# A two-block transformer kernel: expert weights cut across all four experts of a round, in runs of 4 KB, each slot released alone

## What is computed

```python
lg = (xt @ w_rg + b_rg)                      # group logits
g_sel = jnp.argmax(lg, axis=-1)
le = (xt @ w_re + b_re).reshape(t, N_GROUPS, EXPERTS_PER_GROUP)
top_l, top_i = lax.top_k(le_sel, TOP_K_IN_GROUP)
...
return (jax.nn.silu(xblk @ w1[e]) * (xblk @ w3[e])) @ w2[e]
```

## Time and profile before

| | us |
|---|---|
| median of 3 runs | 1914.07 |
| lowest, highest | 1911.24, 1917.08 |
| the profiled execution, its own time | 1911.82 |
| its span in the profile | 1910.1 |
| PE busy, share of the span | 1547.6 (81%) |
| DVE, ACT busy | 424.8 (22%), 248.6 (13%) |
| mean granted TensorE clock | 0.911 |
| HBM read, mean over the span | 708 MB, 371 GB/s |

### The profile page before, as it was taken

How to read it: one execution, slowest core, us unless ns; L and a number is a source line. 1 busy time by engine, 2 the same in 40 slices (tenths; PEclk the granted TensorE clock), 3 DMA queues, 4 the chain that set the end, 5 groups by cost and what they waited for, 6 DMA issues and landing times.

```text
span 1910.1 us, 23311 instructions
## 1 busy us (share of the span) xinstructions
PE 1547.6 (81%) x10212; PEld 745.9 (39%) x10212; DVE 424.8 (22%) x944; ACT 248.6 (13%) x531; POOL 86.8 (5%) x142
## 2 busy tenths in 40 slices
PE   7998777999998778989977667776799677677775
PEld 4754434764454434445522212222255222132222
DVE  2341111326431112463500000000043000000001
ACT  0310000126212011154100000000011000000000
POOL 1100000201100000112100000000000000000000
PEclk9999888999999899999988878888899888778888
DMA  8579999769979999299699999999977999999997
GB/s 288 202 274 423 423 423 416 288 251 388 352 284 416 420 421 413 91 366 383 244 424 423 424 424 423 423 424 424 420 325 315 424 424 424 423 424 424 423 424 288
DMA packets 129039, 711.11 MB, mean 372 GB/s; under 512 B 8377, under 2 KB 14505, under 8 KB 60321
## 3 DMA queue, kind: packets, MB, share of 16 engines
q1 hardware_dynamic: 122512, 697.14, 89.4%
q0 software_dynamic: 4320, 9.78, 1.5%
q10 hardware_dynamic: 2096, 2.57, 0.5%
HBM read 708.17 MB, written 1.05 MB: 371 GB/s over the span
## 4 chain that ended last, share of the span: by engine, by line
PE 46%; DMA 43%; DVE 6%; SPq 2%; ACT 2%; issue 2%; POOL 1%; DVEq 0%; PEldq 0%; ACTq 0%; POOLq 0%
DMA ring<-in_moe_w 23%; DMA ring<-in_moe_w_down 7%; PE pa L820 6%; PE pb L791 5%; DMA work<-in_moe_w 5%; DMA mod<-in_moe_w 4%; PE pa L838 3%; PE pb L768 3%; PE acc L1421 3%; PE acc L893 3%; PE acc L1416 2%; PE acc L1139 2%; DMA ring<-in_moe_w_up 2%; PE acc L1317 2%; DMA work<-in_moe_w_down 2%
## 5 line engine op out<-in xcount | busy, mean ns | idle before, releaser
L791 PE MATMUL pb<-ring,XT 128*32 128x512 f32 x1424 | 271.7, 714 | 89.1 <-DMA ring<-in_moe_w 89.0
L820 PE MATMUL pa<-ring,work 128*32 128x512 f32 x928 | 191.8, 754 | 65.3 <-DMA ring<-in_moe_w 41.5
L791 PEld LDWEIGHTS pb<-ring,XT 128*32 128x32 f32 x1424 | 61.7, 126 | 248.9 <-DMA ring<-in_moe_w 126.2
L838 PE MATMUL pa<-work,HM 128*128 128x128 f32 x1024 | 132.0, 291 | 17.6 <-issue 17.6
L939 DVE TENSOR_TENSOR work<-work,pb 128x256 f32<-128x256 f32 (+1 forms) x32 | 17.7, 554 | 576.1 <-PE pb L791 431.4
L893 PE MATMUL acc<-XT,work 128*128 128x512 f32 x256 | 118.4, 605 | 32.5 <-DVE XT L955 19.6
L838 PEld LDWEIGHTS pa<-work,HM 128*128 128x128 f32 x1024 | 130.5, 207 | 32.4 <-issue 32.4
L791 PE MATMUL pb<-work,XT 128*32 128x512 f32 x480 | 113.8, 697 | 26.4 <-DMA work<-in_moe_w 26.3
L768 PE MATMUL pb<-ring,XT 128*32 128x256 f32 x1600 | 110.2, 398 | 13.8 <-DMA ring<-in_moe_w_up 13.8
L820 PEld LDWEIGHTS pa<-ring,work 128*32 128x32 f32 x928 | 42.8, 132 | 175.8 <-issue 77.3
L902 ACT COPY XT<-pa 128x512 f32<-128x512 f32 x32 | 18.8, 586 | 596.8 <-PE pa L838 596.8
(11 more groups left out here) (416 smaller groups left out, 1795.8 us busy)
## 6 DMA issues: line engine op xcount, KB each, us to landing
ring<-in_moe_w SPq DMA_DIRECT2D x135, 2048.0 KB
work<-in_moe_w SPq DMA_DIRECT2D x46, 2048.0 KB
ring<-in_moe_w_up SPq DMA_DIRECT2D x28, 2048.0 KB
ring<-in_moe_w_gate SPq DMA_DIRECT2D x26, 2048.0 KB
ring<-in_moe_w_down SPq DMA_DIRECT2D x24, 2048.0 KB
ring<-in_w_mod SPq DMA_DIRECT2D x48, 1024.0 KB
mod<-in_moe_w SPq DMA_DIRECT2D x11, 2048.0 KB
work<-in_moe_w_down SPq DMA_DIRECT2D x8, 2048.0 KB
```

What stands on the lines that cost most here:

```text
L791: last = nc.tensor.matmul(hbank[m][j * CAP:(j + 1) * CAP, :], m_xg[:, k, j * CAP:(j + 1) * CAP], slot_of(s0 + j // 2)[:, at:at + fn], star ...
L820: last = nc.tensor.matmul(pa[j * CAP:(j + 1) * CAP, h, :], m_ht[:, c, j * CAP:(j + 1) * CAP], slot_of(i)[:, at:at + 512], start=(c == 0), ...
L838: last = nc.tensor.matmul(xg_ps[:, k, :], HM[:, tt, k * P:(k + 1) * P], m_p[:, tt, :], start=(tt == 0), stop=(tt == TT - 1))
```

## The change

Four edits go together.

1. `across` now holds for every round. Each slot has a quarter-width share of all four experts, four runs of 4 KB in a partition. In the narrow rounds slots 0 and 1 are the two halves of the gate's rows, 2 and 3 of up's, 4 and 5 of down's. In the wide rounds w1 and w3 have two such slots for each half of their rows. Each is waited for and given back by itself. The number and size of the transfers of expert weights stay, and so does the number of matmuls that use them. The extra warm-ups of round 7 stay in round 7 alone.
2. The router's DVE chain: the pick of the second expert and the sum of both picks become one instruction for each tile. The second pick by itself is then the difference, computed behind the release of PE.
3. The warm-ups before the wait for the picks are 10 and not 6.
4. `ab_w_in` comes in whole rows, in halves of a chunk, in order. PE starts with the first half chunk behind 3 warm-ups and waits for each further chunk in its first product.

```diff
 def across(fn, g, i):
     down = moe_slots(fn) - fn // P
-    if g == 0 and i < 2:
-        return 0, 0, i
-    if g == ROUNDS - 1 and i >= down:
+    if i < down:
+        return (i // 2, 0, i % 2) if fn == FN1 else (i // 2 % 2, i // 4, i % 2)
+    if i >= down:
         return 2, (i - down) // 2, (i - down) % 2
...
-            warm_tensor(pe, pb[:, 0, :], 6)
+            warm_tensor(pe, pb[:, 0, :], 10)
...
-                link(v.tensor_scalar(o2[:, t, :], tmp[:, t, :], at_, None, ALU.is_equal))
+                last = v.scalar_tensor_tensor(m_a[:, t, :], tmp[:, t, :], at_, o1[:, t, :], ALU.is_equal, ALU.add)
                 if t == 0:
-                    link(v.tensor_tensor(m_a[:, t, :], o1[:, t, :], o2[:, t, :], ALU.add))
-            v.tensor_tensor(m_a[:, t, :], o1[:, t, :], o2[:, t, :], ALU.add).then_inc(assign_ready, 1)
+                    link(last)
+            last.then_inc(assign_ready, 1)
+            dve.wait_ge(assign_ready, ph.moe + 1)
+            link(v.tensor_tensor(o2, m_a, o1, ALU.subtract))
...
-        def across_up_tensor(fn, rows, s0, bank, wait_full, free, slot_of, n, at_half=None):
-            for k in range(n):
+        def across_up_tensor(fn, rows, s0, k0, bank, wait_full, free, slot_of, n, at_half=None):
+            for k in range(k0, k0 + n):
+                i = s0 + (k - k0) // rows
...
-            if g == ROUNDS - 1:
+            if across(ph.fn, g, n_up):
                 for c in range(n_down):
-                    if c:
+                    if c and g == ROUNDS - 1:
                         warm_tensor(pe, pb[:, 1, :], 8)
...
-            for cols, signal in ((slice(2 * GW, AB_IN), lat_cols), (slice(0, 2 * GW), None)):
...
+            sp.dma_start(dst[:, 0:1, :], src[:, 0:1, :]).then_inc(first_chunk, 16)
+            sp.dma_start(dst[:, 1:2, :], src[:, 1:2, :]).then_inc(full[at[ph.slot0].slot], FILL)
+            stream_sync(sp, a["ab_w_in"][0], ph.slot0, 4, 2, AB_IN, 1)
...
-            pe.wait_ge(lat_cols, 64)
+            warm_tensor(pe, pb[:, 0, :], 3)
+            pe.wait_ge(first_chunk, 16)
             for k in range(KC):
+                if k == 1 or k and k % 2 == 0:
+                    slot_wait(pe, ph.slot0 + k // 2)
```

More of the change, by code:

```diff
@@ L743, in across_up_tensor @@
                 if k % rows == 0:
-                    wait_full(s0 + k // rows)
-                held = slot_of(s0 + k // rows).rearrange("p (j r f) -> p j r f", j=SIDE, r=rows)
+                    wait_full(i)
+                held = slot_of(i).rearrange("p (j r f) -> p j r f", j=SIDE, r=rows)
                 for j in range(SIDE):
@@ L782, in whole_up_tensor @@
                     if across(fn, g, s0):
-                        across_up_tensor(fn, KC // 4, s0, hbank[m], wait_full, free, slot_of, KC // 2)
+                        across_up_tensor(fn, KC // 4, s0, half * KC // 2, hbank[m], wait_full, free, slot_of, KC // 2)
                         continue
@@ L1250, in weights_of, with stream_sync @@
             return w[i * kk * P:(i + 1) * kk * P, cols].rearrange("(k p) c -> p k c", p=P)
-        def stream_sync(sp, w, q0, n, kk, width):
-            for i in range(n):
+        def stream_sync(sp, w, q0, n, kk, width, first=0):
+            for i in range(first, n):
                 dst = slot(q0 + i)[:, 0:kk * width].rearrange("p (k c) -> p k c", k=kk)
@@ L1862, in ab_sync @@
         def ab_sync(sp, ph):
-            for cols, signal in ((slice(2 * GW, AB_IN), lat_cols), (slice(0, 2 * GW), None)):
-                for i in range(4):
-                    q = ph.slot0 + i
-                    dst = slot(q)[:, 0:2 * AB_IN].rearrange("p (k c) -> p k c", k=2)[:, :, cols]
-                    src = weights_of(a["ab_w_in"][0], cols, 2, i)
-                    if signal is None:
-                        sp.dma_start(dst, src).then_inc(full[at[q].slot], FILL)
-                    else:
-                        sp.dma_start(dst, src).then_inc(signal, 16)
+            dst = slot(ph.slot0)[:, 0:2 * AB_IN].rearrange("p (k c) -> p k c", k=2)
+            src = weights_of(a["ab_w_in"][0], slice(0, AB_IN), 2, 0)
+            sp.dma_start(dst[:, 0:1, :], src[:, 0:1, :]).then_inc(first_chunk, 16)
+            sp.dma_start(dst[:, 1:2, :], src[:, 1:2, :]).then_inc(full[at[ph.slot0].slot], FILL)
+            stream_sync(sp, a["ab_w_in"][0], ph.slot0, 4, 2, AB_IN, 1)
             sp.wait_ge(b_small, 16 * B_SMALL)
@@ L1915, in ab_tensor @@
             for k in range(KC):
-                if k % 2 == 0:
-                    slot_wait(pe, ph.slot0 + k // 2)
                 for t in range(TT):
```

9 lines of the change are left out of this document (5 added, 4 removed).

## The result

| | before | after |
|---|---|---|
| median of 4 runs, us | 1912.65 (1908.96 to 1917.08) | 1928.84 (1928.54 to 1929.64) |
| span of the profiled execution, us | 1910.1 | 1927.4 |

The ratio is 1.0091, 95% interval 1.007 to 1.0113: the changed kernel is 16.2 us slower. The forecast was 1932.3, in a range of 1914 to 1946.

A forecast was written before the change was run, and what follows sets the result against it. The prediction took the saturated DMA stream of expert weights to bound the expert phases. Its terms, 25.8 - 0.4 (E1's idle time) - 2.5 - 1.9 - 1.8 - 1.0 = +18.2 us on 1914.07, gave 1932.3 us, range 1914 to 1946.

The forecast's parts named there:

- The bound and the mechanism: Expert phases: a full DMA queue sets their length, and shorter runs lower its rate; forecast chance 0.76.
- The rate: Expert-weight stream: 415 in place of 424 GB/s, 0.107 us more for each of 240 slots, 25.8 us.
- three short stretches: Stretches of 4 KB runs in the kernel before, at 421, 410 and 412 GB/s over 15, 14 and 10 us.
- the 410 and 412 stretches: Kernel before: 410 GB/s is half a mixer's weights, 412 expert weights; all at 410 would cost 41 us.
- The tails: Ends of E0 and E2: single slots let PE finish earlier, 0.6 and 1.9 us, sum -2.5 us.
- my clock rival: Phase ends: PE's bursts bring the lower clock to the tails, about 4 us each, 16 us, so 1948; chance 0.07.
- Parts 2 to 4: Router chain, warm-ups and kernel start: gains of 1.9, 1.8 and 1.0 us.
- the warm-ups' 1.8 us: Router of the wide phases: ten warm-ups shorten PE's idle gap and keep the clock, 0.9 us in each.
- a bracket: Warm-ups term: an aside that E1 and the gather behind may gain too, with no size given.
- The start: First product: starts near 11 us but needs the fourth chunk, so ends near 28.0 us, -1 us.
- The 421 rate: Rival, expert stream: 421 GB/s is the right rate, 8.4 us replace 25.8, so 1914.9, no change; chance 0.10.
- That run length costs nothing: Faster rival, expert stream: 423 GB/s or more in E2 and E3, only 7.2 us of gains, so 1906.9; chance 0.07.

The follow-up runs named there:

- Part 1 alone: Kernel before with only the 4 KB cut across four experts and single release of every expert slot; router, warm-ups and start unchanged: 1937.92 us, ratio 1.0151.
- the 4 KB runs alone: Kernel before with the same slots, experts and paired release, each slot's transfer issued as two so every run is 4 KB: 1942.86 us, ratio 1.0183.
- E2: Not a run: the first wide expert phase of the kernel, 444.92 us long before the change and 454.18 after.
- the rest alone: Changed kernel with the slot cut undone (8 KB runs, two experts); shorter router chain, ten warm-ups and new start stay: 1900.75 us, ratio 0.9957.
- E0: Not a run: the first narrow expert phase of the kernel, 207.44 us long before the change and 212.28 after.
- E3: Not a run: the last expert phase of the kernel, a wide one, 443.63 us long before the change and 453.29 after.
- E1: Not a run: the second narrow expert phase of the kernel, 213.49 us long before the change and 217.09 after.
- e4_16k_last: Kernel before with each slot of the last expert phase filled by one whole matrix in 16 KB runs, outputs differing: 1907.33 us, ratio 0.9974.

## Why the prediction was right

**The bound and the mechanism** held as written. The queue stays full, the rate falls, and the phases lengthen. Part 1 alone and the 4 KB runs alone both show it.

**The rate** was the term that mattered: 25.8 us, from a rate of 415 that I had averaged from three short stretches. Measured was 414. At 414 a slot takes 5.066 us, 0.120 more than at 424, and over the 240 slots that the forecast counted this is 28.8 us. The phases lost 27.4 in all, tails included. The count of the slots was right too: 4.8, 3.6, 9.3 and 9.7 us, where "about 9" and "3 to 4" were forecast. Taking the 410 and 412 stretches as seriously as the 421 one was what made it right. But the rate of 4 KB runs swings between 408 and 422 GB/s within a phase (below), and three short samples of it could have averaged some GB/s more or less. That they came so near to the mean was partly luck.

**The tails** were put too high: 2.5 us forecast. In E2 the way from the last up slot's products to those of the last down slot went from 21.91 to 21.17 us, so 0.7 and not 1.9. The forecast had the last down slot land 20.0 us behind the last up slot, as in the kernel before (20.01 us from arrival to arrival); in the changed one it is 21.18, because the last slot alone takes 6.3 us and not 5.1. It takes 6.2 with the rest alone too, so the run length isn't the reason; what is wasn't tried. E0 gave nothing, since the products of its last up slot and of its first down slot fell to the lower clock: 3.4 us more for both, of which 0.9 reached the end. This is the mechanism of my clock rival, but it cost time in this one place. In E2 and E3 the lower clock reached the first down slot as well, and the last transfer still set the end (waits of 2.26 and 1.00 us); the final additions took 3.70 us in E0, E2 and E3, before and after.

**Parts 2 to 4** were put too low: 4.7 us forecast, 10.0 by the landmarks, 8.2 to 9.7 by the kernel that has them alone. The step that failed is the warm-ups' 1.8 us. I had counted the two places where the trace of before showed slow warm-ups, and left E1's slow gather in a bracket. The runs give 5 to 7 us. Between the traces with six and with ten, 3.2 us are the warm-ups and gathers behind the picks at the lower clock: 1.6 in E0 and 1.6 in E2. The rest of it (with six warm-ups `nsa` is 1.6 us longer, and E0, E1 and E3 are 0.9 to 1.8 us longer behind their gathers) I see between the two traces only, and what links it to the warm-ups stays open. The profiled execution with six was also 2.6 us above its kernel's median. The start gave 1.2 us by its landmark, against 1.0.

**The sum** thus came out 2 us too high (18.2 against 16.2), with two errors that cancel: the phases 4.5 us too low, the rest 5.3 too high by the landmarks. That the sum lies this near is luck: with only one of the two errors it would have missed by about 5 us.

**The rivals.** The 421 rate is out: the mean is 414. That run length costs nothing is out at 414 against 424, and with it the rule of the Trainium skill, page "DMA: Bandwidth & Descriptors", section "Specifications", that 512 B is enough for the full rate. In this queue 8 KB isn't enough either: 16 KB gave 429. The same page's section "Why small descriptors are slow (HBM only)" has the right form, a fixed charge for each packet, but too small a one. Its 3 cycles for each packet, beside 256 for the 8 KB, give an estimate of 1.2% from 8 to 4 KB and 0.6% from 16 to 8. Measured were 2.4% and 1.2%.

## What to carry to other kernels

Where a full DMA queue sets the time, count the bytes of each contiguous run before anything else: halving it from 8 to 4 KB cost 2.4% of the rate, doubling it gave 1.2%. Buy finer slots with shorter runs only where a phase begins or ends and the slot is really waited for, and keep the long runs in between. Before idle time is filled with finer work, ask when the last transfer lands, and whether the engine's clock survives the gaps that this makes.

## What the runs showed of the hardware

**A run costs a fixed time.** In the DMA records the transfers of 8 KB take 309 to 314 ns each on their engine, those of 4 KB 159 to 164. A straight line through both has some 10 ns beside the bytes. The 16 KB ones (e4_16k_last) take 611 ns in the median, where the line through the medians of the other two, 159 and 309 ns, gives 609.

**The rate depends on where the slot lies.** In the slices of E2 above (part 1 alone, 9.2 us each) the rate peaks nine times, from the fourth to the 39th slice, so every 40 us: the time of eight slots, and E2 uses eight. In E3, which uses nine, the same kernel has slices of 9.5 us with eight peaks from the third to the 37th, every 46 us:

```profile
GB/s 413 412 422 413 409 410 416 419 412 409 410 419 421 409 409 409 421 417 409 410 410 418 413 411 407 413 421 415 410 409 415 420 413 410 408 417 421 411 409 410
```

A wide round has 12 slots, so the period is that of the places and not of the matrices. In the packets of the changed kernel, sorted by place, six of E3's nine places are filled in about 5.13 us and three in 5.00; with 8 KB runs, before, it was 4.98 and 4.91. Stretches of 10 to 15 us cover two or three places, which can explain why the kernel before showed 421, 410 and 412 GB/s. Why some places are slower wasn't tried.

**Products to the same 32 rows don't overlap.** With 32 columns of weights each, 512 wide, they took 0.76 us apiece in a row, and 0.24 when four row groups took turns, both at a granted clock of 1.00.

**The clock can fall after short idle times.** Behind 1.35 us of idle time ahead of the picks the next 16 products ran at the lower clock, and so did the next 8 behind a 2.16 us wait at an end. It doesn't follow from the gap alone: 1.34 to 2.12 us ahead of the picks were followed by slow products in 13 of 20 cases, 0.43 to 0.80 us in none of 32. Warm-ups that begin when the clock is already low run slowly themselves: 16 records took 3.79 us in place of 2.05.
